# One loop for scan, z product and output product in the SSD layer of a two-layer transformer kernel

## The chip, the cores and the metric

The kernel runs on one core of one Trainium2 chip, for one sequence of 256 tokens with model width 2048, all data in 32 bit. The metric is the device time of one execution in microseconds (us), the median of several. The engines are TensorE (PE in the profile), VectorE (DVE), ScalarE (ACT), GpSimd (POOL), and the queue that starts the weight loads (SP).

## What is computed

Two layers follow each other: an attention layer with a Fourier part, then an SSD (state space) layer, a sparse attention layer on top of it and layer norms between. Only the SSD layer is touched. Its reference, cut:

```
def ssd_mixer(x, w_in, conv_w, conv_b, dt_bias, a_log, d_skip, norm_g, w_out):
    z, xbc, dt = jnp.split(x @ w_in, [4096, 4096 + 6144], -1)
    xs, bm, cm = split(silu(causal_depthwise_conv(xbc, conv_w, conv_b)))
    xs = xs.reshape(b, L, g, r, p)                 # 8 groups x 8 heads x 64
    dt = softplus(dt + dt_bias); a = -exp(a_log)
    y = ssd_chunked(xs, dt, a, bm, cm, chunk)      # one chunk of 256 tokens
    y = y + d_skip[..., None] * xs
    yg = (y * silu(z)).reshape(b, L, g, 512)
    yg = yg * rsqrt(mean(yg * yg, -1) + 1e-6)      # per group
    return (yg.reshape(b, L, 4096) * norm_g) @ w_out

def ssd_chunked(...):                              # with one chunk only y_diag is left
    cb = einsum('bclgn,bcsgn->bgcls', cc, bc)
    y_diag = einsum('bgcls,bgrcls,bcsgrp->bclgrp', cb, exp(segsum(dt * a)), xs * dt)
```

z (2048 to 4096 columns) needs only x; the scan of a group needs its x, B, C and dt columns; the output product of a group needs the scan and z of that group. So there are, for each of 8 groups, three pieces of work: one z block, one scan, one output block.

## The kernel before

Every weight matrix is streamed through SBUF once. A **tile** is 1 MB (512 rows by 512 columns) in one of four `raw` buffers, and has two **units** of 256 rows. Since TensorE multiplies in a shortened format, each unit is split into a high part `w_hi` (ScalarE, L402) and a low part `w_lo` (VectorE, L924), and TensorE does three products for each chunk: high by high, low by high, high by low (L1650 to L1652, 12 matmuls of 512 columns to a unit). Four units fit in `w_hi` and `w_lo`, so the split of unit u waits for `units_used` of u-4, and TensorE's unit u waits for `lo_done` of u. TensorE's order of work is written out by hand, and so are the orders of ScalarE and VectorE: between their own steps they are told to split so many units `ahead`, and each engine takes its instructions strictly in that order.

The stretch of interest has these stages:
- **dt product** (L1944) and, at its end, the z product: 8 blocks of 4 tiles (`z_block`, L1984), each 8 units, into PSUM banks 0 and 1 or 2 and 3 by turns. ScalarE reads each block with Silu (L718) into `gatedf`, where z of all 8 groups is kept.
- **scan loop** (`scan_turn`, L2013 on TensorE, L745 on ScalarE, L1303 on VectorE, `stage_scan`, L1609 on GpSimd), 8 turns. Turn g does the scan of group g and the output product of group g-1 (`out_tile`, four tiles of two units). On TensorE: the product C by B (`cb`, L2017, L2018), output tiles 0 and 1, the SSD product y (L2030 to L2032, 24 small matmuls, each done in two passes), output tiles 2 and 3, eight transposes of the normed y (L2042).
- after it four output tiles of group 7, and the layer norm.

Around y of group g stands a chain. ScalarE makes the decay factors in two halves, each 8 Relu instructions (L738) and one Exp of 1536 columns (L743); VectorE masks them (L1315) and weights x with dt (L1321) and with d_skip (L1333). When y is in PSUM, VectorE adds and gates it (L1342, L1345), ScalarE squares and sums (L757), VectorE forms the mean (L1348), ScalarE the root (L761), VectorE its inverse (L1350), ScalarE scales (L765), TensorE transposes, ScalarE and VectorE store the high and the low part (L771, L1356). VectorE also adds each output tile from PSUM to the residual x (`add_out`, L1301); out tile n may begin only after tile n-2 was added, for it has the same two banks. GpSimd brings the cumulated sums (`r`, a DMA of 1 MB broadcast, L1611) and stages the columns of B (L1618). ScalarE loads another function table when it goes from Silu or Sqrt to Exp and so on (ACT_TABLE_LOAD).

Of the kernel before, what the change touches and what calls it, by code (L numbers as in the profile page):

```python
# [83 lines left out]

def make_tables():
# [35 lines left out]
def tile_list():  # L121
# [16 lines left out]
    blocks("ssd_z", 8, 4)  # L138
    blocks("ssd_out", 32, 1)
# [12 lines left out]
def build(nc, a, out, acs_dram):  # L152
# [21 lines left out]
    for seg, _, _, _, _ in TILES:  # L174
        if seg not in ("head_q", "head_kv") and all(seg != s for s, _ in BLOCKS):
# [25 lines left out]
    with ExitStack() as ctx:  # L201
# [51 lines left out]
        def tile_source(seg, b, j):  # L253
# [88 lines left out]
        def _(sp):  # L342
# [50 lines left out]
        def _(e):  # L393
# [294 lines left out]
            def dt_splits(u0):  # L688
# [3 lines left out]
                e.activation(tx[0:64, 0:256], ps[0:64, 4, 0:256], ACT.Identity, bias=sm[0:64, 65:66]).then_inc(S["dt_act"], 1)  # L692
# [9 lines left out]
            def z_two(i):  # L702
                for k in range(2):
                    ahead = 2 * FIRST["ssd_z"] + 8 * k + 4
                    if k == 0 and isinstance(i, int):
                        dt_splits(ahead)
                    elif isinstance(i, int):

                        splits(ahead, 4)
                        e.activation(x[:, :, :], x[:, :, :], ACT.Copy, scale=ALPHA).then_inc(S["x_scaled"], 1)  # L710
                        splits(ahead + 4, 4)
                    else:
                        splits(ahead, 8, i, 16)
                    b = 2 * i + k
                    e.wait_ge(units_used, ready("ssd_z", b))
                    for n in range(2):
                        fixed()
                        e.activation(gatedf[:, ds(b * 1024 + LO + n * 512, 512)], ps[:, 2 * k + n, :],  # L718
                                     ACT.Silu).then_inc(act_freed if n == 1 else S["half_read"], 1)
            each(e, 4, z_two)  # L720


            ex = actf[:, 1024:4096]
            rb = actf[:, 5120:7168]
            U0 = 2 * FIRST["ssd_out"]
            e.wait_ge(units_used, ready("ssd_z", 7))
# [18 lines left out]
            def scan_turn(g):  # L745
                def ahead(m):
                    if not isinstance(g, int) or g > 0:
                        split(U0 - 8 + m, g, 8)

                decay(g, 1)  # L750
                for m in range(4, 8):
                    ahead(m)
# [22 lines left out]
                if not isinstance(g, int) or g < G - 1:  # L775
                    decay(g + 1, 0)
# [141 lines left out]
        def _(e):  # L918
# [384 lines left out]
            def scan_turn(g):  # L1303
                def ahead(m):
                    if not isinstance(g, int):
                        split(U0 - 8 + m, g, 8)

# [900 lines left out]
```

## Time and profile before

| | us |
|---|---|
| median of 3 runs | 2343.94 |
| lowest and highest | 2336.14 and 2345.91 |
| span of the profiled execution (first to last instruction) | 2338.8 |

The profile is that of one execution. For each engine it gives the busy time, the instructions in order of time with the wait before them and what ended it, and the clock that was granted to TensorE. "Idle" in brackets behind an instruction is the time its engine stood still before it, with the instruction that it waited for; "issue" is a wait for which the profile shows no releaser. The stretch from the first z unit to the last output unit goes from 1214.5 to 1671.4 us after the span's start, 456.9 us.

### The profile page before, as it was taken

The numbers are of one execution on the slowest core, as the hardware profiler recorded it, in microseconds if no ns is written. First come the engines' busy times: TensorE is split into PE (matmuls) and PEld (weight loads), VectorE is DVE, ScalarE is ACT, GpSimd is POOL, SyncE is SP. The second block draws the span as 40 slices with busy tenths as digits, with TensorE's granted clock in tenths as the row PEclk, the third lists the DMA queues.
The fourth block names the chain that finished last, engine by engine and source line by source line (L and its number), as shares of the span: only waits on it lengthen the run. The fifth ranks groups of instructions, "written<-read, shape, count | busy, mean of one in ns | idle before, by whom it ended". The sixth has DMA issues, their size and how long they took to land.

```text
span 2338.8 us, 33230 instructions
## 1 busy us (share of the span) xinstructions
PE 2144.7 (92%) x13270; PEld 1913.9 (82%) x13270; DVE 1359.4 (58%) x1772; ACT 1138.1 (49%) x1526; POOL 38.9 (2%) x60
## 2 busy tenths in 40 slices
PE   4989999999999998999999978999799998888996
PEld 3768898789999887999988867787698998776885
DVE  5864755444665555666664445777755544665454
ACT  5832445544553344444435446667454345564333
POOL 0000000000000000000000000010000000000000
PEclk8889999999999999999999998999899999999998
DMA  9933533335785554555545552445354554223652
GB/s 350 334 137 107 192 133 109 108 127 182 269 285 183 180 190 143 181 167 179 166 154 191 189 196 101 157 173 180 113 177 136 166 186 138 88 90 125 198 191 79
DMA packets 204233, 394.62 MB, mean 169 GB/s; under 512 B 6726, under 2 KB 25916, under 8 KB 201692
## 3 DMA queue, kind: packets, MB, share of 16 engines
q1 hardware_dynamic: 199584, 369.78, 47.4%
q0 software_dynamic: 2880, 17.40, 2.0%
q10 hardware_dynamic: 1660, 5.90, 0.6%
q8 instruction: 79, 1.29, 0.2%
q14 instruction: 30, 0.25, 0.0%
HBM read 390.89 MB, written 2.16 MB: 168 GB/s over the span
## 4 chain that ended last, share of the span: by engine, by line
PE 71%; ACT 10%; DVE 10%; issue 6%; DMA 1%; ACTq 1%; DVEq 0%; POOL 0%; POOLq 0%
PE ps L1662 11%; PE ps L1664 11%; PE ps L1663 11%; PE ps L1650 10%; PE ps L1651 10%; PE ps L1652 10%; ACT w_hi L402 4%; DVE w_lo L924 3%; ACT actf L738 2%; PE ps L1732 1%; PE ps L1733 1%; DMA tables<-in_tables 1%; ACT actf L859 1%; PE ps L1824 1%; DVE sm L1489 1%
## 5 line engine op out<-in xcount | busy, mean ns | idle before, releaser
L924 DVE TENSOR_TENSOR w_lo<-raw,w_hi 128x1024 fp32r<-128x1024 f32 (+1 forms) x708 | 850.3, 1220 | 765.5 <-ACT w_hi L402 764.9
L402 ACT ACTIVATE w_hi<-raw 128x1024 fp32r<-128x1024 f32 (+1 forms) x708 | 730.1, 1052 | 738.8 <-PE ps L1664 368.0
L1662 PE MATMUL ps<-act,w_hi 128*128 128x256 f32 x2048 | 587.3, 287 | 5.1 <-DVE w_lo L924 3.8
L1664 PE MATMUL ps<-act,w_lo 128*128 128x256 f32 x2048 | 580.8, 284 | 0.0
L1663 PE MATMUL ps<-act,w_hi 128*128 128x256 f32 x2048 | 580.7, 284 | 0.0
L1662 PEld LDWEIGHTS ps<-act,w_hi 128*128 128x128 f32 x2048 | 393.1, 192 | 9.6 <-DVE w_lo L924 4.6
L1663 PEld LDWEIGHTS ps<-act,w_hi 128*128 128x128 f32 x2048 | 393.0, 192 | 2.9 <-issue 2.2
L1664 PEld LDWEIGHTS ps<-act,w_lo 128*128 128x128 f32 x2048 | 392.9, 192 | 0.0
L1650 PE MATMUL ps<-w_hi,act 128*128 128x512 f32 (+1 forms) x896 | 354.1, 395 | 23.7 <-DVE act L1356 12.6
L1651 PE MATMUL ps<-w_lo,act 128*128 128x512 f32 (+1 forms) x896 | 349.3, 390 | 0.0
L1652 PE MATMUL ps<-w_hi,act 128*128 128x512 f32 (+1 forms) x896 | 349.2, 390 | 0.0
L1650 PEld LDWEIGHTS ps<-w_hi,act 128*128 128x128 f32 x896 | 170.2, 190 | 61.8 <-issue 25.7
L1651 PEld LDWEIGHTS ps<-w_lo,act 128*128 128x128 f32 x896 | 170.5, 190 | 34.4 <-issue 0.7
L1652 PEld LDWEIGHTS ps<-w_hi,act 128*128 128x128 f32 x896 | 170.1, 190 | 34.7
L1650 PE MATMUL ps<-w_hi,gated 128*128 128x512 f32 x320 | 126.7, 396 | 1.4 <-DVE gated L1520 1.4
L1651 PE MATMUL ps<-w_lo,gated 128*128 128x512 f32 x320 | 125.8, 393 | 0.0
L1652 PE MATMUL ps<-w_hi,gated 128*128 128x512 f32 x320 | 125.7, 393 | 0.0
L1732 PE MATMUL ps<-w_hi,gated 128*128 128x512 f32 x128 | 60.1, 469 | 21.9 <-DVE w_lo L924 21.8
L1662 PE MATMUL ps<-gated,w_hi 128*128 128x256 f32 x256 | 72.5, 283 | 3.7 <-DVE w_lo L924 3.7
L1650 PEld LDWEIGHTS ps<-w_hi,gated 128*128 128x128 f32 x320 | 61.0, 191 | 14.4 <-DVE gated L1520 1.6
L1663 PE MATMUL ps<-gated,w_hi 128*128 128x256 f32 x256 | 72.4, 283 | 0.0
L1664 PE MATMUL ps<-gated,w_lo 128*128 128x256 f32 x256 | 72.4, 283 | 0.0
(285 smaller groups left out, 2446.1 us busy)
## 6 DMA issues: line engine op xcount, KB each, us to landing
raw<-in_ssd_w_in SPq DMA_DIRECT2D x80, 1024.0 KB, 5.1
raw<-in_w_in SPq DMA_DIRECT2D x72, 1024.0 KB, 5.1
raw<-in_w_ada SPq DMA_DIRECT2D x48, 1024.0 KB, 5.8
raw<-in_dsa_w_in SPq DMA_DIRECT2D x36, 1024.0 KB, 5.0
raw<-in_ssd_w_out SPq DMA_DIRECT2D x32, 1024.0 KB, 5.0
raw<-in_dsa_w_out SPq DMA_DIRECT2D x32, 1024.0 KB, 5.1
raw<-in_w_out SPq DMA_DIRECT2D x16, 1024.0 KB, 5.1
raw<-in_w_proj_a SPq DMA_DIRECT2D x12, 1024.0 KB, 5.1
```

The lines of the kernel that those rows point to most:

```text
L402: e.activation(w_hi[:, u % SPLIT, :, :w], raw[:, t % RAW, 2 * h:2 * h + 2, :w], ACT.Copy).then_inc(hi_done, 1)
L738: ins = e.activation(ex[:, o:o + w], rb[:, h * 256 + tt * 128:h * 256 + 256], ACT.Relu, scale=-1.0, bias=sm[:, 76 + tt * 8 + h:77 + tt * 8 ...
L859: e.activation(v, v, ACT.Exp, bias=sm[:, c + 2 + tt:c + 3 + tt], scale=ATT_SCALE, accum_out=sm[:, c + 4 + tt:c + 5 + tt]).then_inc(S["hs_e ...
L924: e.tensor_tensor(w_lo[:, u % SPLIT, :, :w], raw[:, t % RAW, 2 * h:2 * h + 2, :w], w_hi[:, u % SPLIT, :, :w].bitcast(F32), ALU.subtract).t ...
L1489: e.tensor_reduce(sm[:, c + tt:c + 1 + tt], p[:, lo:hi], AX_X, ALU.max).then_inc(S["hs_step"], 1)
L1650: e.matmul(ps[:, bank, :w], hi, w_hi[:, slot, c, :w], start=first, stop=False)
L1651: e.matmul(ps[:, bank, :w], hi, w_lo[:, slot, c, :w], start=False, stop=False)
L1652: ins = e.matmul(ps[:, bank, :w], lo, w_hi[:, slot, c, :w], start=False, stop=last)
L1662: e.matmul(o, wh, hi, start=first and f % 2 == 0, stop=False, skip_group_check=True)
L1663: e.matmul(o, wh, lo, start=False, stop=False, skip_group_check=True)
L1664: ins = e.matmul(o, wl, hi, start=False, stop=last and f % 2 == 1, skip_group_check=True)
L1732: e.matmul(ps[:, bank + 2 * k, :], cols[:, kc, :], w_hi[:, slot, c, :], start=kc == 0, stop=False)
```

## The change

The 8 z blocks are no longer done ahead of the scan. Only z of groups 0 and 1 is (segment `ssd_z`, 2 blocks); then a loop of six turns (g = 1 to 6, two to a pass) does the scan of group g, the z block of group g+1 and the output product of group g-1, with one new run of weight tiles (`ssd_zo`: four z tiles, four output tiles); group 7's scan and the last two output products follow. z is kept for two groups only (`ZS`), and the room of the others takes the decay factors (`EX`), the broadcast sums (`RB`) and the low parts of y (`YL`). z is now always in banks 4 and 5, y in 6 and 7, `cb` in bank 0, which output tiles 0 and 2 have too. No arithmetic is added or left out. The same splits, products and DMAs are done; their order is another, and so is what each stands behind. New helper names are `z_silu`, `y_squares`, `y_root`, `y_scale`, `y_high` on ScalarE, `masked`, `weighted`, `y_gated`, `y_mean`, `y_rstd`, `y_low` on VectorE, and `group_products`, `y_product`, `y_turn` on TensorE: each holds the step of that name that the loop before had written out. `splits(u, n)` splits n units from u on.

The core of the diff:

```diff
+ZS = LO
+EX = LO + 2048
+RB = LO + 5120
+YL = 28
...
-    blocks("ssd_z", 8, 4)
-    blocks("ssd_out", 32, 1)
+    blocks("ssd_z", 2, 4)
+    blocks("ssd_zo", 6, 8)
+    blocks("ssd_out", 8, 1)
...
+            def scan_loads(i):
+                n0 = FIRST["ssd_zo"]
+                for j in range(4):
+                    load(n0 + j, i, i, 8)
                 for t in range(4):
-                    n = FIRST["ssd_out"] + t
-                    sp.wait_ge(lo_done, 2 * (n - RAW) + 2 + 8 * g)
-                    sp.dma_start(raw[:, n % RAW:n % RAW + 1, :, :],
-                                 w[:, ds(g, 1), :, t * CB:(t + 1) * CB]).then_inc(raw_landed[n % RAW], 16)
-            each(sp, G, out_group)
+                    out_tile(n0 + 4 + t, i, t, i, 8)
+            each(sp, 6, scan_loads)
+            for t in range(8):
+                out_tile(FIRST["ssd_out"] + t, 6 + t // 4, t % 4, 0, 0)
...
+            dt_splits(Z0 + 4)
+            z_silu(0, ready("ssd_z", 0))
+            splits(Z0 + 12, 4)
             decay(0, 0)
-            each(e, G - 1, scan_turn)
-            scan_turn(G - 1)
-            splits(U0 + 60, 8)
+            e.activation(x[:, :, :], x[:, :, :], ACT.Copy, scale=ALPHA).then_inc(S["x_scaled"], 1)
+            splits(Z0 + 16, 2)
+            decay(0, 1)
+            splits(Z0 + 18, 2)
+            z_silu(1, ready("ssd_z", 1))
+            y_squares(0)
+            y_root(0)
+            y_scale(0)
+            decay(1, 0)
+            decay(1, 1)
+            def scan_turn(g, k, i):
+                def ahead(m, n=1):
+                    splits(ZO + 16 * k + m, n, i, 32)
+                ahead(4, 4)
+                y_high(g - 1)
+                ahead(8, 4)
+                z_silu(k, ZO + 16 * k + 8 + 32 * i)
+                y_squares(g)
+                ahead(12)
+                y_root(g)
+                ahead(13)
+                y_scale(g)
+                ahead(14)
+                decay(g + 1, 0)
+                ahead(15)
+                ahead(16)
+                decay(g + 1, 1)
+                ahead(17, 3)
+            def scan_two(i):
+                scan_turn(2 * i + 1, 0, i)
+                scan_turn(2 * i + 2, 1, i)
+            each(e, 3, scan_two)
+            y_high(6)
+            splits(U0 + 4, 2)
+            y_squares(7)
+            y_root(7)
+            y_scale(7)
+            splits(U0 + 6, 4)
+            y_high(7, 4)
+            splits(U0 + 10, 10)
...
+            dt_splits(Z0 + 4)
+            splits(Z0 + 12, 8)
+            e.wait_ge(S["xt_copied"], 8)
+            e.wait_ge(S["acs_stored"], 16)
+            masked(0, 0)
+            masked(0, 1)
+            weighted(0)
+            y_gated(0, 0)
+            y_mean(0)
+            y_rstd(0)
+            e.wait_ge(S["x_scaled"], 1)
...
+            def scan_turn(g, k, i):
+                def ahead(m, n=1):
+                    splits(ZO + 16 * k + m, n, i, 32)
+                def add(t):
+                    e.wait_ge(units_used, ZO + 16 * k + 10 + 2 * t + 32 * i)
+                    e.wait_ge(dve_freed, out_freed(4 * g - 8 + t))
+                    v = x[:, :, t * 512:(t + 1) * 512]
+                    e.tensor_tensor(v, ps[:, 2 * (t % 2):2 * (t % 2) + 2, :], v, ALU.add).then_inc(dve_freed, 1)
+                masked(g, 0)
+                masked(g, 1)
+                ahead(4, 4)
+                weighted(g)
+                y_low(g - 1)
+                ahead(8, 4)
+                y_gated(g, (k + 1) % 2)
+                ahead(12)
+                y_mean(g)
+                ahead(13)
+                add(0)
+                y_rstd(g)
+                ahead(14, 2)
+                add(1)
+                ahead(16, 2)
+                add(2)
+                ahead(18, 2)
                 add(3)
...
+            masked(7, 0)
+            masked(7, 1)
+            weighted(7)
+            y_low(6)
+            splits(U0 + 4, 2)
+            y_gated(7, 1)
+            y_mean(7)
+            add_last(24)
+            y_rstd(7)
+            splits(U0 + 6, 2)
+            add_last(25)
+            splits(U0 + 8, 2)
+            add_last(26)
+            y_low(7, 4, 0)
+            splits(U0 + 10, 2)
+            add_last(27)
...
+            e.wait_ge(S["dt_ready"], 1)
+            e.wait_ge(S["xt_copied"], 8)
...
+            pair_free(BI["ssd_z"])
+            gemm(Z0, 8, act, 4, True)
+            turn_dt()
+            group_products(0)
+            e.wait_ge(act_freed, z_freed(0))
+            gemm(Z0 + 8, 8, act, 4, True)
+            y_product(0)
+            def scan_turn(g, k, i):
+                u0 = ZO + 16 * k
+                e.wait_ge(dve_freed, out_freed(4 * g - 6))
+                group_products(g)
+                e.wait_ge(act_freed, z_freed(g))
+                gemm(u0, 4, act, 4, True, i, 32, ends=False)
+                y_turn(g - 1)
+                gemm(u0 + 4, 4, act, 4, True, i, 32, kc0=8, starts=False)
+                y_product(g)
+                for t in range(4):
+                    out_tile(t, g - 1, u0 + 8, i, 32)
+            def scan_two(i):
+                scan_turn(2 * i + 1, 0, i)
+                scan_turn(2 * i + 2, 1, i)
+            each(e, 3, scan_two)
+            e.wait_ge(dve_freed, out_freed(22))
+            group_products(7)
+            y_turn(6)
+            y_product(7)
+            for t in range(3):
+                out_tile(t, 6, U0, 0, 0)
+            y_turn(7)
+            out_tile(3, 6, U0, 0, 0)
             for t in range(4):
-                out_tile(t, G)
+                out_tile(t, 7, U0 + 8, 0, 0, 4, 0)```

How it moves instructions, at three places.

On VectorE, the turn before from the gating of y to the third addition to x (L1345 gating, L924 `w_lo`, L1348 mean, L1350 inverse root, L1301 addition):

```order
L1345 TENSOR_TENSOR tables<-tables,gatedf 128x1024
L923 REGISTER_ALU
L924 TENSOR_TENSOR w_lo<-raw,w_hi 128x1024
L1347 ISA
L1348 TENSOR_SCALAR sm<-sm 128x2
L1349 REGISTER_ALU
L1350 RECIPROCAL sm<-sm 128x2
L923 REGISTER_ALU
L924 TENSOR_TENSOR w_lo<-raw,w_hi 128x1024
L1298 ISA
L1299 REGISTER_ALU
L1301 TENSOR_TENSOR x<-ps,x 128x2x512
```

and the turn now, from the gating (L1366) to the third addition (L1405 the addition, L980 `w_lo`, L1370 mean, L1374 inverse root):

```order
L1366 TENSOR_TENSOR tables<-tables,gatedf 128x1024
L980 TENSOR_TENSOR w_lo<-raw,w_hi 128x1024
L1370 TENSOR_SCALAR sm<-sm 128x2
L980 TENSOR_TENSOR w_lo<-raw,w_hi 128x1024
L1405 TENSOR_TENSOR x<-ps,x 128x2x512
L1374 RECIPROCAL sm<-sm 128x2
L980 TENSOR_TENSOR w_lo<-raw,w_hi 128x1024 x2
L1405 TENSOR_TENSOR x<-ps,x 128x2x512
L980 TENSOR_TENSOR w_lo<-raw,w_hi 128x1024 x2
L1405 TENSOR_TENSOR x<-ps,x 128x2x512
```

Before, two of the four additions stood ahead of the gating; now all four stand behind it, with six of the turn's `w_lo` among them.

On ScalarE, the turn before from behind the scaling of y to the next group's decay (L402 `w_hi`, L771 high part of y, L738 first Relu of the decay):

```order
L401 REGISTER_ALU
L402 ACTIVATE w_hi<-raw 128x1024
L767 REGISTER_ALU
L770 REGISTER_ALU
L771 ACTIVATE act<-ps,sm 128x256 x4
L401 REGISTER_ALU
L402 ACTIVATE w_hi<-raw 128x1024
L401 REGISTER_ALU
L402 ACTIVATE w_hi<-raw 128x1024
L731 ISA
L732 REGISTER_ALU
L738 ACTIVATE actf<-actf,sm 128x256
```

and now (L779 scaling, L433 `w_hi`, L756 Relu, L761 Exp):

```order
L779 ACTIVATE tables<-tables,sm 128x512 x2
L433 ACTIVATE w_hi<-raw 128x1024
L756 ACTIVATE gatedf<-gatedf,sm 128x256
...
L756 ACTIVATE gatedf<-gatedf,sm 128x128
L761 ACT_TABLE_LOAD
L761 ACTIVATE gatedf<-gatedf 128x1536
L433 ACTIVATE w_hi<-raw 128x1024 x2
L756 ACTIVATE gatedf<-gatedf,sm 128x256
```

The decay's first half came behind all of a turn's output units; now it stands between unit 14 and unit 15 of the turn's 16, and the second half between the first and the second unit of the next turn.

On TensorE, before, the end of the first z block (L1952 the transposes of dt, then z of the second):

```order
L1650 MATMUL ps<-w_hi,act 128x512
L1651 MATMUL ps<-w_lo,act 128x512
L1652 MATMUL ps<-w_hi,act 128x512
L1952 MATMUL ps<-tables 128x64 x4
L1650 MATMUL ps<-w_hi,act 128x512
```

and now (L2043 the transposes, L2085 and L2086 `cb` of group 0, L1741 z of group 1):

```order
L1743 MATMUL ps<-w_hi,act 128x512
L2043 MATMUL ps<-tables 128x64 x4
L2085 MATMUL ps<-side,tables 128x256
L2086 MATMUL ps<-side,tables 128x128
L1741 MATMUL ps<-w_hi,act 128x512
```

The product `cb` of group 0 came behind the eighth z block; now it comes ahead of the second one.

## Rows read from the trace of the kernel before

**Rows 1.** The page: busy time of the engines, and the chain that ended last.
```profile
PE 2144.7 (92%) x13270; PEld 1913.9 (82%) x13270; DVE 1359.4 (58%) x1772; ACT 1138.1 (49%) x1526; POOL 38.9 (2%) x60
...
PE 71%; ACT 10%; DVE 10%; issue 6%; DMA 1%; ACTq 1%; DVEq 0%; POOL 0%; POOLq 0%
```

**Rows 2.** Windows: length; busy PE, PEld, DVE, ACT, POOL; granted clock; DMA share, GB/s.
```profile
1214.50:1389.50 175.00, 174.99 (x773) 144.32 (x772) 82.25 (x74) 82.24 (x85) 0.56 (x1) 1.00 0.56 183
1389.50:1423.60 34.10, 15.15 (x64) 14.27 (x64) 11.41 (x13) 18.02 (x35) 4.36 (x7) 0.55 0.31 110
1423.60:1647.30 223.70, 208.57 (x1089) 177.12 (x1088) 164.31 (x170) 158.83 (x268) 16.71 (x27) 0.98 0.46 159
```

**Rows 3.** TensorE in order of time: start, length, instruction, idle before and its releaser.
```profile
1402.89 0.66 PE L2030 MATMUL ps<-actf 128*128 128x64 f32 x2 [7.95 <-DVE actf L1315]
...
1434.79 0.33 PE L2030 MATMUL ps<-actf 128*128 128x64 f32 x2
...
1440.06 0.48 PE L1650 MATMUL ps<-w_hi,act 128*128 128x512 f32 x1
...
1451.16 1.10 PE L2042 MATMUL ps<-tables 128*128 128x128 f32 x8
1452.09 0.60 PE L2017 MATMUL ps<-side,tables 128*128 x2
...
1455.37 0.49 PE L1650 MATMUL ps<-w_hi,act 128*128 128x512 f32 x1 [2.45 <-DVE act L1356]
...
1484.10 0.60 PE L2017 MATMUL ps<-side,tables 128*128 x2
```

**Rows 4.** ScalarE in order of time, from the squares of group 1.
```profile
1445.53 0.60 ACT L757 ACTIVATE ps<-tables 128x512 f32<-128x512 f32 x1 [8.52 <-DVE tables L1345]
...
1447.98 1.28 ACT L761 ACT_TABLE_LOAD   x1
...
1449.77 1.34 ACT L765 ACTIVATE tables<-tables,sm 128x512 f32<-128x512 f32 x2 [0.23 <-DVE sm L1350]
...
1455.28 2.88 ACT L738 ACTIVATE actf<-actf,sm 128x256 f32<-128x256 f32 x8
1458.17 1.28 ACT L743 ACT_TABLE_LOAD   x1
1459.47 1.49 ACT L743 ACTIVATE actf<-actf 128x1536 f32<-128x1536 f32 x1
1460.86 2.86 ACT L738 ACTIVATE actf<-actf,sm 128x256 f32<-128x256 f32 x8
...
1465.15 3.88 ACT L402 ACTIVATE w_hi<-raw 128x1024 fp32r<-128x1024 f32 x4
```

**Rows 5.** VectorE: the gating in order of time, then groups of 1452 to 1484.
```profile
1442.92 1.21 DVE L1342 TENSOR_TENSOR tables<-ps,tables 128x1024 f32<-128x1024 f32 x1
...
L924 DVE TENSOR_TENSOR w_lo<-raw,w_hi 128x1024 fp32r<-128x1024 f32 x8 | 9.5, 1216 | 4.8 <-ACT w_hi L402 4.8
L1301 DVE TENSOR_TENSOR x<-ps,x 128x1024 f32<-128x1024 f32 x4 | 4.9, 1214 | 0.0
L1315 DVE TENSOR_TENSOR actf<-actf,t 128x1536 f32<-128x1536 f32 x2 | 3.5, 1770 | 2.5 <-ACT actf L743 2.4
```

**Rows 6.** GpSimd in order of time: the first staging of B.
```profile
1390.06 0.59 POOL L1611 DMA_DIRECT2D actf<-acs_dram  x1 [159.80 <-PE ps L1652]
...
1391.84 1.39 POOL L1618 COPY tables<-side 128x256 f32<-128x256 f32 x1
```

**Rows 7.** VectorE's copy of dt, and ScalarE's scaling of x, in order of time.
```profile
1238.83 0.42 DVE L1273 COPY t<-ps 128x256 f32<-128x256 f32 x1
...
1249.06 3.61 ACT L710 ACTIVATE x<-x 128x4096 f32<-128x4096 f32 x1
```

**Rows 8.** Busy time and granted clock behind a wait of 2.46 us; columns as Rows 2.
```profile
1488.00:1490.00 2.00, 2.00 (x8) 1.60 (x7) 2.00 (x3) 2.00 (x7) 1.01 (x1) 0.70 0.95 371
1490.00:1492.00 2.00, 2.00 (x6) 1.52 (x6) 2.00 (x3) 1.97 (x3) 0.00 (x0) 0.50 0.27 30
```

More of the change, by code:

```diff
@@ L174, in build @@
     for seg, _, _, _, _ in TILES:
-        if seg not in ("head_q", "head_kv") and all(seg != s for s, _ in BLOCKS):
+        if seg == "ssd_zo" and all(seg != s for s, _ in BLOCKS):
+            for _ in range(6):
+                BLOCKS.append((seg, "act"))
+                BLOCKS.extend([(seg, "dve")] * 4)
+        elif seg not in ("head_q", "head_kv") and all(seg != s for s, _ in BLOCKS):
             nb = 1 + max(t[1] for t in TILES if t[0] == seg)
@@ L183, in build, with z_freed, out_freed @@
         BI.setdefault(seg, n)
+    Z_FREED = sum(1 for seg, who in BLOCKS[:BI["ssd_z"]] if who == "act")
+    OUT_FREED = sum(1 for seg, who in BLOCKS[:BI["ssd_z"]] if who == "dve")
+    def z_freed(b):
+        return Z_FREED + 1 + b
+    def out_freed(n):
+        return OUT_FREED + 1 + n
     def freed_count(engine, n):
@@ L282, in tile_source @@
                 return [(0, 4, rows(a["ssd_w_in_2"], k0, b * CB))]
+            if seg == "ssd_zo" and j < 4:
+                return [(0, 4, rows(a["ssd_w_in_2"], k0, b * CB + 2 * CB))]
             if seg == "lat_q":
@@ L700, in dt_splits, with z_silu @@
                 splits(u0 + 2, 6)
[L702 to L724, printed above, removed]
-            U0 = 2 * FIRST["ssd_out"]
-            e.wait_ge(units_used, ready("ssd_z", 7))
+            Z0 = 2 * FIRST["ssd_z"]
+            ZO = 2 * FIRST["ssd_zo"]
+            U0 = 2 * FIRST["ssd_out"]
+            ex = gatedf[:, EX:EX + 3072]
+            rb = gatedf[:, RB:RB + 2048]
+            def z_silu(k, used):
+                e.wait_ge(units_used, used)
+                for n in range(2):
+                    e.activation(gatedf[:, ZS + k * 1024 + n * 512:ZS + k * 1024 + (n + 1) * 512], ps[:, 4 + n, :],
+                                 ACT.Silu).then_inc(act_freed if n == 1 else S["half_read"], 1)
             def decay(g, n):
@@ L743, in decay, with y_squares @@
                 e.activation(part, part, ACT.Exp, scale=-1.0).then_inc(S["decay_ready"], 1)
[L745 to L752, printed above, removed]
+            def y_squares(g):
                 e.wait_ge(S["y_step"], 4 * g + 2)
@@ L1272, in dt_splits @@
                 e.wait_ge(S["dt_turned"], 1)
-                e.tensor_copy(t1[:, :], ps[:, 5, 0:256]).then_inc(S["dt_ready"], 1)
-            def z_two(i):
-                for k in range(2):
-                    ahead = 2 * FIRST["ssd_z"] + 8 * k + 4
-                    if k == 0 and isinstance(i, int):
-                        dt_splits(ahead)
-                    else:
-                        splits(ahead, 8, i, 16)
-            each(e, 4, z_two)
-            e.wait_ge(act_freed, freed("ssd_z", 7))
@@ L1303, in scan_turn @@
[L1303 to L1306, printed above, removed]
-                def add(t):
-                    if not isinstance(g, int):
-                        add_out(t, g)
-                def masked(n):
-                    e.wait_ge(S["decay_ready"], 2 * g + n + 1)
-                    v = ex[:, n * 1536:(n + 1) * 1536].rearrange("p (h l) -> p h l", h=4)
-                    e.tensor_tensor(v, v, cbm.unsqueeze(1).to_broadcast([P, 4, 384]), ALU.mult).then_inc(S["m_ready"], 1)
+                e.tensor_copy(t1[:, :], ps[:, 7, 0:256]).then_inc(S["dt_ready"], 1)
@@ L2013, in scan_turn, with group_products @@
[L2013 to L2014 removed]
+            Z0 = 2 * FIRST["ssd_z"]
+            ZO = 2 * FIRST["ssd_zo"]
+            U0 = 2 * FIRST["ssd_out"]
+            ex = gatedf[:, EX:EX + 3072]
+            bst = tx[:, 1024:1280]
+            def group_products(g):
                 e.wait_ge(S["b_staged"], g + 1)
                 e.wait_ge(S["cb_masked"], g)
[L2017 to L2018 removed]
+                e.matmul(ps[:, 0, 0:256], bst[:, 0:P], side[:, ds(256 * g + 2048, 256)], start=True, stop=True)
+                e.matmul(ps[:, 0, 256:384], bst[:, P:2 * P], side[:, ds(256 * g + 2048 + P, P)],
```

184 lines of the change are left out of this document (81 added, 103 removed).

## The prediction

> **What bounds the kernel now.** I read the page first, then busy time by windows, then the engines in order of time around the scan loop. On the page [rows 1] TensorE is busy for 92% of the span and is 71% of the chain that ended last: the reader is to see that only time in which TensorE waits, or runs at its lower clock, can be won or lost by a new order, since the change leaves all products as they are. The windows [rows 2] say where that time is. In the z blocks TensorE waits for nothing (174.99 of 175.00 us, clock 1.00): 8 blocks at 21.8 us, a unit (an eighth) 2.72 us. In the first scan turn (1389.5 to 1423.6) it works 15.2 of 34.1 us at a clock of 0.55; in the seven turns behind it 208.6 of 223.7 us. Output tiles are 12 matmuls to a unit like z, so 2.72 us too.
>
> A turn's own scan work on TensorE at full clock is y, 5.27 us (1434.79 to 1440.06), transposes 0.93 us (1451.16 to 1452.09), and `cb` about 0.87 us (from 1452.09 to the start of the 2.45 us of idleness ahead of 1455.37) [rows 3]: 7.07 us in all. From the first z unit to the last output unit there are 456.9 us; the work in it is 16 x 21.76 + 8 x 7.07 + 0.4 for dt = 405.1. **So 51.8 us are waits and half clock**: 34.1 - 7.1 = 27 in the first turn, 25 in the rest (a turn takes 32.0 us, 1452.09 to 1484.10 [rows 3], for 28.8 of work). The change can win at most these 51.8 us, and must not make others.
>
> **The chain of a turn now.** Let y of group g end at 0 on TensorE. I add what stands in ScalarE's and VectorE's queues, in the new order.
> - Gating, two VectorE instructions: from 1442.92 until ScalarE's squares at 1445.53 [rows 4, 5]: 2.6, so 2.7 with the hand-over.
> - Squares 1.4 (1445.53 to the split behind them): 4.2. `w_hi` 1.0: 5.2. Table load and root 1.6: 6.8. `w_hi` 1.0: 7.8.
> - Now VectorE: the new order has `w_lo` and addition 0 ahead of the inverse root, 1.14 each start to start (a row mean is 1.21 with its overlap [rows 5]), and 0.2: 10.3. Before, the inverse root followed at once (scaling began 1.79 after the load's start [rows 4]).
> - ScalarE: scaling 1.3, `w_hi` 1.0: 12.6. First half of the next decay 5.58 (1455.28 to 1460.86 [rows 4]): 18.2. `w_hi` of unit 15: 19.2. VectorE: `w_lo` of unit 15, then addition 1: **21.5**.
> - Output tile 3 has the banks of tile 1 and waits for addition 1. TensorE did tiles 0 to 2 in 6 x 2.72 = 16.3, so it **waits 5.2 us**. Tile 3 ends at 27.0.
> - ScalarE goes on: `w_hi` 20.2, second half of the decay 4.29 (1460.86 to 1465.15 [rows 4]) 24.5, `w_hi` 25.5; VectorE `w_lo`, addition 2: 27.8. The next `cb` uses bank 0 and waits for addition 2: **0.8 us** more.
> - Then TensorE has `cb` 0.87, a z block 21.76, transposes 0.93, y 5.27, with all units split in time (ScalarE needs 1.0 and VectorE 1.14 for one, TensorE 2.72): 28.8. The turn takes 27.8 + 28.8 = **56.6 us**.
>
> Before, the same two blocks and one scan took 32.0 + 21.8 = 53.8. TensorE's own work would be 50.6. So the z block does cover the transposes and the parts of y, but its cover lies on the wrong side: ScalarE is free during the z block and overbooked in the output tiles, where two decay halves and six splits queue behind the root. Six turns have 6 x 6.0 = 36.0 us of waits. Added up the same way, the old loop's turn comes to 32.2 us against 32.0 measured, so the sum is good to some tenths of a us in a turn.
>
> **Start.** z of group 0 ends at 1236.3 as before; dt's transposes are at 1236.7. `cb` of group 0 now stands ahead of z of group 1 and waits for the copy of dt (ends 1239.25 [rows 7]) and then GpSimd's first staging, 3.1 us (1390.06 to 1393.2 [rows 6]): until 1242.3, a wait of 5.5 us. Cover for it there is none. z of group 1 ends at 1264.9. VectorE must do 8 `w_lo` before it masks group 0, and the last of them wait for ScalarE, which from 1255.2 (split of unit 15) does decay 5.6, scaling of x 3.6 [rows 7], 2 splits, decay 4.3, 2 splits: 1272.6. Then `w_lo` 1.2, mask of `cb` 0.6, two masks at 1.7, two weightings at 1.14: 1280.2. y of group 0 **waits 15.4 us**. In turn 1 the units 4 to 7 of z come behind both decay halves of group 1 (ScalarE: root and scaling done 7.2 after y, decays 9.9, split 1.0, VectorE a mask 1.7 and `w_lo` 1.1: 20.9 from y to the unit), while TensorE has `cb`, four units and the transposes, 12.7, and some tenths of hand-over: **7.2 us**.
>
> **End.** `cb` 7 and the transposes of group 6 take 1.8 us, and no z block follows: VectorE still has two `w_lo`, addition 3, masks, weightings and low parts, so y of group 7 **waits 9.4 us** (from 1.8 to 11.2 behind `cb`: addition 2 at 0, 2 x 1.14, 1.14, 0.6, 3.4, 2.3, 1.6). Output tile 2 then waits 2.4 us for addition 24, which stands behind the gating, two splits and the mean.
>
> **Sum of waits at full clock:** 5.5 + 15.4 + 7.2 + 36.0 + 9.4 + 2.4 = 75.9 us.
>
> **Clock.** No row shows these waits, so I bound their clock from both sides. The nearest rows: behind 2.46 us of idleness the clock was 0.70 and then 0.50 in two windows of 2 us [rows 8], which costs 2 x (0.30 + 0.50) = 1.6 us, and 1.7 with the piece behind; behind 2.45 us at 1455.37 it stayed full [rows 2, 3]. And y of group 0, after 7.95 us of idleness, ran throughout at the half clock (its first step is 0.66 against 0.33), so 5.3 us more than 5.27. Least: the waits of 7 us and more alone fall to half, 2 x 5.3 for y of groups 0 and 7. Most: each wait costs 1.7 more. I take the upper end, since 5.2 us is twice the 2.46 that did cost it: start `cb` and z 2.5; y 0 with `cb` and z behind it 7.9; turn 1 1.7; in five more turns 1.7 less the 0.8 of slack that tile 3 has before addition 2, and a little for the second tile, 1.1 each, 5.5; y 7 and output 7.0. Sum **24.6** (least 10.6).
>
> A page of the Trainium skill, TensorE: Matmul & The Clock Gate, section "HAM oscillation — how this bites in real kernels", says that a loop with a wait in each iteration can find the clock fallen in each. By that rule all six turns would pay; by the rows about half did in the old loop.
>
> **Result.** Waits and half clock 75.9 + 24.6 = 100.5 against 51.8: **48.7 us slower**. The profiled execution's 2338.8 becomes 2387.5; the median shown is 5.1 above that span, so 2343.9 + 48.7 = **2392.6 us**. Silu's table load in each turn, the DMA (the same tiles in 56.6 us, each landing in about 5), and the copy of `r`, asked for some 19 us ahead, cost nothing: ScalarE is idle for 3.7 us before the squares, and the loads have two free buffers ahead.
>
> **Rivals.**
> 1. *The clock holds in the loop* (as at 1455.37): losses are 10.6 instead of 24.6: 2378.6, and 2368.0 with no loss at all. For it: half the old gaps lost nothing. Against it: these are twice as long. Chance 0.20, centred on 2379.
> 2. *The loop runs at TensorE's pace*, not slower than before: the place is addition 1 of VectorE; it decides by whether it is there 16.3 us after y, where I have 21.5. Then 36.0 and the 5.5 of clock in it are gone: 2392.6 - 41.5 = 2351.1, no change. For it: ScalarE and VectorE are busy some 34 of 50 us of a turn, so there is room on average. Against it: ScalarE's and VectorE's queues are in order, and each link of the 21.5 has its row. Chance 0.09.
> 3. *The same, and the clock holds too*: 75.9 - 36.0 = 39.9 against 51.8, 11.9 faster, 2332.0; and less if the start's 15.4 is shorter. Chance 0.08.
> 4. *Each table change costs more than its row.* On the chain there are two loads a turn (root, Exp). The row of a load is 1.28 and the next instruction starts 0.01 behind it (1458.17 to 1459.47 [rows 4]). If another 1.4 us, the length of the Exp's row, came with each of them, 16.8 in six turns would give 2409. The rows of both loads stand in the turn already, so 0.03.
>
> The Trainium skill's page ScalarE: Activation LUTs, section "What ACT_TABLE_LOAD costs", gives 1283 ns and a drain of some 1380 ns for each change of set; by it rival 4 would be the forecast. The trace agrees with the first figure and shows no second.
>
> **Chances.** The forecast has 0.60 (its own range 2383 to 2402), rivals 0.20, 0.09, 0.08, 0.03. Half a per cent, 11.7 us, is about what the measurement of this kernel tells from no change. Faster by more: rival 3, of which half lies at the limit and part of rival 2's spread, 0.08; within it: rival 2 and the rest, 0.10; slower 0.82. The range leaves out rival 3, part of rival 2 and what is above 2409: 2350 to 2409.
>
> **What would show it.** In the profile after: a turn of about 57 us from `cb` to `cb`; in each, TensorE idle by some 5 us before output tile 3, released by VectorE's addition to x, and again a little before `cb`; idle of 5.5 us behind z of group 0, of 15 us before y of group 0, of 9 before y of group 7; y of groups 0 and 7 at half clock. If tile 3 starts without a wait, the chain above is wrong and rival 2 or 3 holds. If the turn is 56 to 57 and the granted clock is 1.00 in the loop, rival 1. If ScalarE stands still behind a table load, rival 4.

## The result, and the profile after

The changed kernel takes 2395.1 us (median; 2393.75 to 2396.02), the kernel before, run beside it, 2344.9 us: a ratio of 1.0219, with a 95% interval of 1.0196 to 1.0241. It is slower by 50 us. The forecast was 2392.6 us.

Busy time of the engines on the page after, which answers to [rows 1]:

```profile
PE 2167.7 (91%) x13270; PEld 1932.6 (81%) x13270; DVE 1359.5 (57%) x1772; ACT 1148.6 (48%) x1533; POOL 36.2 (2%) x60
```

The same 13270 matmuls and 1772 VectorE instructions, and seven more on ScalarE (table loads). TensorE's 23.0 us more busy time at an equal count are matmuls at the lower clock. The rest of the loss is idleness, and the list of TensorE's waits from 1200 to 1760 us names it (engine, line, what it waited for: us in total, times, longest):

```profile
PE ps L1741 <- DVE x L1405: 29.6, 6, 5.0
PE ps L2100 <- DVE gatedf L1357: 15.2, 1, 15.2
...
PE ps L2100 <- DVE gated L1380: 10.0, 1, 10.0
PE ps L1741 <- DVE w_lo L980: 6.3, 1, 6.3
...
PE ps L2085 <- POOL tables L1709: 4.0, 1, 4.0
...
PE ps L1741 <- DVE x L1437: 2.2, 1, 2.2
```

L1741 is the first of a unit's products, L1405 and L1437 VectorE's additions to x, L2100 y, L2085 `cb`. From top to bottom these are: output tile 3 behind addition 1 in each of six turns; y of group 0 behind its weighting; y of group 7 behind the low parts of group 6; the fifth z unit of turn 1; `cb` of group 0 behind GpSimd's staging; output tile 2 of group 6.

Windows over the changed stretch, with the columns of [rows 2] (z of group 0; from there to y of group 0; y of group 0 and turn 1; turns 2 to 6, up to `cb` of group 7; the end):

```profile
1218.50:1241.00 22.50, 22.50 (x100) 18.05 (x98) 13.35 (x17) 11.38 (x14) 0.56 (x1) 1.00 0.38 121
1241.00:1286.00 45.00, 25.77 (x105) 20.83 (x106) 17.43 (x15) 27.11 (x35) 2.31 (x7) 0.80 0.51 175
1286.00:1363.90 77.90, 66.73 (x301) 57.03 (x302) 34.26 (x35) 46.71 (x76) 2.03 (x4) 0.83 0.29 96
1363.90:1653.20 289.30, 264.49 (x1262) 221.29 (x1261) 170.84 (x166) 170.92 (x250) 12.69 (x20) 0.94 0.49 165
1653.20:1725.00 71.80, 59.63 (x261) 50.27 (x259) 43.55 (x47) 24.04 (x32) 1.24 (x3) 0.83 0.44 149
```

Before, TensorE stood full and at a clock of 1.00 for 175 us of this stretch [rows 2]; after, only z of group 0 is so, and every other window has idleness and a clock below 1. From the first z unit to the last output unit there are now 506.1 us (1218.9 to 1725.0), against 456.9: **49.3 us more, where 48.7 was worked out**. The spans differ by 55.3; the other 6 us lie outside the changed stretch, 4.4 of them before it begins.

One turn, turn 2, in TensorE's order of time (`cb` of group 2, output tile 3, and `cb` of group 3):

```profile
1363.89 0.59 PE L2085 MATMUL ps<-side,tables 128*128 128x256 f32 x2
...
1414.01 0.80 PE L1741 MATMUL ps<-w_hi,gated 128*128 128x512 f32 x1 [4.84 <-DVE x L1405]
...
1421.46 0.59 PE L2085 MATMUL ps<-side,tables 128*128 x2
```

A turn is 57.6 us here, 57.8 to 58.0 in the four behind it. Tile 3 waited 4.84 us and took 7.45 us instead of 5.44, for it began at half clock (0.80 for its first product where 0.49 is usual). ScalarE in the same turn, from the squares:

```profile
1395.30 0.60 ACT L768 ACTIVATE ps<-tables 128x512 f32<-128x512 f32 x1 [4.37 <-DVE tables L1366]
...
1397.75 1.28 ACT L773 ACT_TABLE_LOAD   x1
...
1402.76 1.34 ACT L779 ACTIVATE tables<-tables,sm 128x512 f32<-128x512 f32 x2 [2.50 <-DVE sm L1374]
...
1404.95 2.87 ACT L756 ACTIVATE gatedf<-gatedf,sm 128x256 f32<-128x256 f32 x8
1407.84 1.28 ACT L761 ACT_TABLE_LOAD   x1
1409.13 1.48 ACT L761 ACTIVATE gatedf<-gatedf 128x1536 f32<-128x1536 f32 x1
1410.52 1.99 ACT L433 ACTIVATE w_hi<-raw 128x1024 fp32r<-128x1024 f32 x2
```

and VectorE behind it:

```profile
1411.59 1.23 DVE L980 TENSOR_TENSOR w_lo<-raw,w_hi 128x1024 fp32r<-128x1024 f32 x1 [5.29 <-ACT w_hi L433]
1412.74 1.22 DVE L1405 TENSOR_TENSOR x<-ps,x 128x1024 f32<-128x1024 f32 x1
```

Read from below: tile 3 starts at 1414.01, addition 1 ends at 1413.96, it stood behind the low split of unit 15, which stood behind the high split of unit 15, which stood behind the first half of the next group's decay, which stood behind the scaling, which waited 2.50 us for the inverse root, which stood behind a split and addition 0. No step of this is late because its work takes long; each is late for its place in a queue.

### The profile page after: what moved, and what is told of

It is laid out like the page before. It is cut to its first block, busy times and chain, and to the rows that moved or that the text cites. A ratio compares the mean times of both kernels' runs of the same rounds, so it can differ in the third digit from the quotient of the medians.

```text
span 2394.1 us, 32966 instructions
## 1 busy us (share of the span) xinstructions
PE 2167.7 (91%) x13270; PEld 1932.6 (81%) x13270; DVE 1359.5 (57%) x1772; ACT 1148.6 (48%) x1533; POOL 36.2 (2%) x60
## 3 DMA queue, kind: packets, MB, share of 16 engines
q8 instruction: 86, 1.41, 0.2%
## 4 chain that ended last, share of the span: by engine, by line
PE 72%; DVE 11%; ACT 10%; issue 5%; DMA 2%; ACTq 0%; DVEq 0%; POOL 0%; POOLq 0%; SPq 0%
PE ps L1753 11%; PE ps L1755 11%; PE ps L1754 11%; PE ps L1741 10%; PE ps L1742 10%; PE ps L1743 10%; ACT w_hi L433 4%; DVE w_lo L980 2%; ACT gatedf L756 1%; PE ps L1823 1%; DMA tables<-in_tables 1%; PE ps L1824 1%; ACT actf L915 1%; PE ps L1915 1%; PE ps L2100 1%
## 5 line engine op out<-in xcount | busy, mean ns | idle before, releaser
L980 DVE TENSOR_TENSOR w_lo<-raw,w_hi 128x1024 fp32r<-128x1024 f32 (+1 forms) x708 | 850.9, 1220 | 822.2 <-ACT w_hi L433 821.6
L433 ACT ACTIVATE w_hi<-raw 128x1024 fp32r<-128x1024 f32 (+1 forms) x708 | 731.4, 1051 | 797.1 <-PE ps L1743 403.2
L1741 PE MATMUL ps<-w_hi,act 128*128 128x512 f32 (+1 forms) x640 | 254.7, 398 | 13.7 <-issue 7.4
L1741 PE MATMUL ps<-w_hi,gated 128*128 128x512 f32 x576 | 234.7, 407 | 33.3 <-DVE x L1405 29.6
L1742 PE MATMUL ps<-w_lo,act 128*128 128x512 f32 (+1 forms) x640 | 250.8, 392 | 0.0
L1743 PE MATMUL ps<-w_hi,act 128*128 128x512 f32 (+1 forms) x640 | 250.5, 391 | 0.0
L1742 PE MATMUL ps<-w_lo,gated 128*128 128x512 f32 x576 | 231.0, 401 | 0.0
L1743 PE MATMUL ps<-w_hi,gated 128*128 128x512 f32 x576 | 230.3, 400 | 0.0
L1741 PEld LDWEIGHTS ps<-w_hi,gated 128*128 128x128 f32 x576 | 112.8, 196 | 59.9 <-issue 21.6
L1741 PEld LDWEIGHTS ps<-w_hi,act 128*128 128x128 f32 x640 | 123.0, 192 | 40.4 <-issue 10.0
L1743 PEld LDWEIGHTS ps<-w_hi,act 128*128 128x128 f32 x640 | 122.6, 192 | 25.1
L1742 PEld LDWEIGHTS ps<-w_lo,act 128*128 128x128 f32 x640 | 122.7, 192 | 24.7 <-issue 0.7
L1743 PEld LDWEIGHTS ps<-w_hi,gated 128*128 128x128 f32 x576 | 112.3, 195 | 24.6
L1742 PEld LDWEIGHTS ps<-w_lo,gated 128*128 128x128 f32 x576 | 112.9, 196 | 23.3
L1823 PE MATMUL ps<-w_hi,gated 128*128 128x512 f32 x128 | 59.9, 468 | 22.0 <-DVE w_lo L980 22.0
L1753 PE MATMUL ps<-gated,w_hi 128*128 128x256 f32 x256 | 73.3, 286 | 3.7 <-DVE w_lo L980 3.7
```

Source lines behind the costliest of these rows:

```text
L433: e.activation(w_hi[:, u % SPLIT, :, :w], raw[:, t % RAW, 2 * h:2 * h + 2, :w], ACT.Copy).then_inc(hi_done, 1)
L980: e.tensor_tensor(w_lo[:, u % SPLIT, :, :w], raw[:, t % RAW, 2 * h:2 * h + 2, :w], w_hi[:, u % SPLIT, :, :w].bitcast(F32), ALU.subtract).t ...
L1741: e.matmul(ps[:, bank, :w], hi, w_hi[:, slot, c, :w], start=first, stop=False)
L1742: e.matmul(ps[:, bank, :w], hi, w_lo[:, slot, c, :w], start=False, stop=False)
L1743: ins = e.matmul(ps[:, bank, :w], lo, w_hi[:, slot, c, :w], start=False, stop=last)
L1753: e.matmul(o, wh, hi, start=first and f % 2 == 0, stop=False, skip_group_check=True)
```

## The experiments

Each is the changed kernel with one thing moved (the last has all). "Stretch" is from the first z unit to the last output unit in the profile, 506.1 us in the changed kernel and 456.9 before; it leaves out what lies outside the change. The ratio is to the kernel before. Line numbers shift by some lines where a run's kernel is shorter or longer. Outside the stretch all ten kernels do the same work, and it took 1879.1 to 1888.0 us of the profiled spans, the most in the changed kernel; no run shows why. So the medians below fell by 2 to 7 us more than the stretches, and most of them lie under what was expected: the theories are read from the stretch and the turns.

**The decay last (e1).** ScalarE's loop:

```diff
-                ahead(14)
-                decay(g + 1, 0)
-                ahead(15)
-                ahead(16)
-                decay(g + 1, 1)
-                ahead(17, 3)
+                ahead(14, 6)
+                decay(g + 1, 0)
+                decay(g + 1, 1)
```

> Only ScalarE's order in the loop changes: both halves of the next group's decay come behind the turn's last split (unit 19) instead of between units 14, 15, 16 and 17. Theory (the turn is set by ScalarE's and VectorE's queues between y and the additions 1 and 2): addition 1 is there about 16 us after y, output tile 3 starts without a wait, the decays run while TensorE does the next z block, and only about 1.2 us of wait is left at the fifth z unit. A turn goes from 57.9 to about 51.8 us, the kernel to about 2362 us. Rival A (TensorE's two banks and the handing over of them cost the 5 us, whatever ScalarE does): the wait before tile 3 stays, about 2395. Rival B (the decays then come too late for y, and y waits for the masks): the turn stays at 57 to 58.

Measured: 2360.1 us, ratio 1.007 (1.0051 to 1.0088). Stretch 474.0, 32.1 less. A turn is 52.2 to 52.3 us. TensorE's waits:

```profile
PE ps L2097 <- DVE gated L1377: 15.3, 1, 15.3
PE ps L2097 <- DVE gatedf L1354: 15.2, 1, 15.2
PE ps L1738 <- DVE w_lo L977: 13.6, 6, 6.3
```

(L2097 is y here, L1738 the first of a unit's products.) The wait for the addition to x is gone from the list: the two banks alone cost nothing, so rival A falls. A smaller one, for the low split of the fifth z unit, stands in its place (13.6 us in six turns, 6.3 of them turn 1's as before), and y of group 7 waits 15.3 instead of 10.0, for its decay now comes later. Rival B falls as well.

**The inverse root first (e2).** VectorE's loop:

```diff
+                y_rstd(g)
                 ahead(13)
                 add(0)
-                y_rstd(g)
```

> Only VectorE's order in the loop changes: the inverse root stands right behind the mean, ahead of the low split of unit 13 and addition 0. ScalarE's scaling of y can start 2.3 to 2.5 us sooner. Theory (a chain on which every instruction counts): the turn goes from 57.9 to about 55.0 to 55.5 us, the kernel to about 2377 to 2380 us. Rival (only the decay's place counts, or there is slack in front of the scaling): a gain below 5 us.

Measured: 2369.9 us, ratio 1.011 (1.0092 to 1.0129). Stretch 486.5, 19.6 less; a turn 54.7 to 54.9. Moving one instruction of 0.15 us takes 3.1 us off a turn. What TensorE still waits for before tile 3:

```profile
PE ps L1741 <- DVE x L1405: 14.0, 6, 2.4
```

ScalarE's wait of 2.50 us for the inverse root is gone, and with it 2.5 us of the turn; the other 0.6 fit a shorter half clock. The clock still falls in each of the six turns, behind waits of 2.23 to 2.39 us, but tile 3 then works at half for 3.2 to 3.6 us and not for 4.1 to 4.6. The expectation was 2377 to 2380 us, 15 to 18 less; the stretch gives 19.6 and the median 25.2.

**Addition 1 between the splits (e3).**

```diff
-                ahead(14, 2)
+                ahead(14)
                 add(1)
+                ahead(15)
                 ahead(16, 2)
```

> Only VectorE's order changes: addition 1 stands between the low splits of units 14 and 15, so output tile 3 need not wait for the split of unit 15 to have its banks. Theory (two chains of equal length: behind addition 1 comes addition 2, which needs the second half of the decay and sets the next product of C and B): the wait before tile 3 falls below 1 us, and comes back in front of unit 15 and of the next turn's first product; turn 57.5 to 58, kernel 2394 to 2397 us. Rival (the wait for the banks is what costs): 5 us less a turn, kernel about 2365 us.

Measured: 2390.3 us, ratio 1.0203 (1.0183 to 1.0224). Stretch 506.5, the same within 0.4 us. Turns 2 to 6 take 59.2 us falling to 57.8, where 57.5 to 58 was expected, and turn 1 and the last group are shorter by as much. The waits have only changed places:

```profile
PE ps L2086 <- DVE x L1405: 27.1, 6, 4.7
PE ps L2101 <- DVE gatedf L1357: 15.2, 1, 15.2
PE ps L1742 <- DVE w_lo L980: 12.5, 7, 6.3
```

L2086 is `cb`: it now waits 27.1 us for addition 2, where tile 3 had waited 29.6 for addition 1; tile 3 waits 1.0 to 1.1 us, for the low split of unit 15. So there are two chains of nearly equal length, as the prediction had it, and releasing one gives nothing.

**Idle products in the wait (e4).**

```diff
-                for t in range(4):
+                for t in range(3):
                     out_tile(t, g - 1, u0 + 8, i, 32)
+                e.wait_ge(act_freed, z_freed(g + 1))
+                for n in range(16):
+                    e.matmul(ps[:, 4, :], act[:, 0, n, 0:P], act[:, 0, 0:2, :], start=True, stop=True)
+                out_tile(3, g - 1, u0 + 8, i, 32)
```

> TensorE gets 16 idle products (512 columns, their result is not used) ahead of output tile 3 in each of the six turns, 3.6 us in a wait of 5.0. Theory (the half clock in the loop costs about 1.2 us a turn beyond the 56.6 of the queues): the granted clock stays at 1.00 in the turns, a turn takes about 56.7 us, the kernel about 2388 us. Rival (the turn's 57.9 is the queues' own length and the clock is without effect, since tile 3 has slack): no change, 2395 us. If the idle products themselves delay tile 3: slower than 2395.

Measured: 2382.2 us, ratio 1.0162 (1.0143 to 1.0181): 12.9 us under the changed kernel's time, 8.7 in the stretch. A turn is 56.5 to 56.8 us. Windows around the wait, the changed kernel above and this one below (the third column from the right is the granted clock):

```profile
1409.00:1413.00 4.00, 0.17 (x1) 0.00 (x0) 1.41 (x2) 3.99 (x6) 0.00 (x0) 0.77 0.01 2
1413.00:1417.00 4.00, 3.00 (x7) 2.44 (x8) 2.08 (x2) 3.97 (x9) 0.00 (x0) 0.50 0.73 221
```
```profile
1406.00:1410.00 4.00, 4.00 (x19) 3.16 (x17) 0.99 (x1) 3.99 (x5) 0.00 (x0) 1.00 0.01 2
1410.00:1414.00 4.00, 2.78 (x12) 2.12 (x12) 2.50 (x3) 3.97 (x9) 0.00 (x0) 1.00 0.61 183
```

```profile
1468.30 0.49 PE L1741 MATMUL ps<-w_hi,gated 128*128 128x512 f32 x1 [1.38 <-DVE x L1405]
...
1474.70 0.69 PE L2085 MATMUL ps<-side,tables 128*128 x2 [0.66 <-DVE x L1405]
```

With work that nobody needs, the granted clock stays at 1.00 from turn 2 to turn 6, and TensorE shows what the queues alone make: behind the idle products a wait of 1.2 to 1.4 us is left before tile 3, and one of 0.4 to 0.7 before `cb`, which is the second chain's wait that the slow tile 3 had hidden. The half clock in the loop was worth 0.9 to 1.5 us a turn, 1.2 on average: 57.6 to 58.0 against 56.5 to 56.8. Of the 8.7 us of the stretch 5.9 are those five turns and 0.8 tile 3 of turn 1; the other 2.0 lie where nothing was changed, most of them at the fifth z unit of turn 1, which worked at half clock for 3.3 us instead of 6.3.

**The start's order (e5).** ScalarE and VectorE ahead of the loop:

```diff
-            splits(Z0 + 12, 4)
+            splits(Z0 + 12, 3)
             decay(0, 0)
-            e.activation(x[:, :, :], x[:, :, :], ACT.Copy, scale=ALPHA).then_inc(S["x_scaled"], 1)
-            splits(Z0 + 16, 2)
+            splits(Z0 + 15, 1)
             decay(0, 1)
+            splits(Z0 + 16, 2)
+            e.activation(x[:, :, :], x[:, :, :], ACT.Copy, scale=ALPHA).then_inc(S["x_scaled"], 1)
             splits(Z0 + 18, 2)
...
-            splits(Z0 + 12, 8)
+            splits(Z0 + 12, 3)
             e.wait_ge(S["xt_copied"], 8)
             e.wait_ge(S["acs_stored"], 16)
+            weighted(0)
+            splits(Z0 + 15, 1)
             masked(0, 0)
             masked(0, 1)
-            weighted(0)
+            splits(Z0 + 16, 4)
```

> Only the start changes, ahead of the loop. ScalarE does the two halves of group 0's decay behind the third and fourth split of the second z block, and the scaling of x behind them; VectorE weights group 0 and masks it before the low splits of units 16 to 19. Theory (y of group 0 waits 15.2 us for ScalarE's and VectorE's order, not for data): that wait nearly goes (below 3 us), and with it some of the half clock: about 18 us less, 2377 us. Rival (the wait is the arrival of the broadcast sums or of dt): the wait stays at 10 us or more.

Measured: 2375.4 us, ratio 1.0128 (1.0107 to 1.0149); stretch 489.4, 16.8 less. The wait of 15.2 us before y of group 0 has gone from the list of waits; one of 2.1 us for Silu's reading of banks 4 and 5 has come behind it, before z of group 2. The 15.2 us were order alone.

**`cb` of group 0 in the middle of the second z block (e6).**

```diff
-            group_products(0)
             e.wait_ge(act_freed, z_freed(0))
-            gemm(Z0 + 8, 8, act, 4, True)
+            gemm(Z0 + 8, 4, act, 4, True, ends=False)
+            group_products(0)
+            gemm(Z0 + 12, 4, act, 4, True, kc0=8, starts=False)
```

> Only TensorE's order at the start changes: the product of C and B of group 0 stands in the middle of the second z block instead of ahead of it. Theory: the 8 us between z of group 0 and this product go, but 3 us of them come back as the wait for Silu's reading of the same banks, and the next wait, before y of group 0, takes the rest except what it gained, so the end moves only by about 3 to 6 us: 2389 to 2392 us. Rival (waits add up, nothing gives back): 8 to 10 us less, 2386.

Measured: 2392.0 us, ratio 1.0211 (1.0194 to 1.0228); stretch 504.8, 1.3 less where 3 to 6 was expected; no difference from the changed kernel that the times can tell. From the first z unit to `cb` of group 1 it is 2.6 us shorter (74.6 for 77.2), and the rest is longer again by about half of that. The 4.0 us for GpSimd are gone, and the waits behind it are 3.2 us for Silu's reading of banks 4 and 5 and 14.5 instead of 15.2 before y. A wait that is followed by a longer one on another queue was worth almost nothing by itself here.

**The decay in its own turn's z block (e7).** ScalarE, and VectorE's masks likewise:

```diff
-                ahead(4, 4)
+                decay(g, 0)
+                ahead(4)
+                decay(g, 1)
+                ahead(5, 3)
                 y_high(g - 1)
...
-                ahead(14)
-                decay(g + 1, 0)
-                ahead(15)
-                ahead(16)
-                decay(g + 1, 1)
-                ahead(17, 3)
+                ahead(14, 6)
```

> The decay of group g moves from the output tiles of the turn before into its own turn's z block, its halves on both sides of the split of unit 4, and VectorE's masks likewise. Theory: TensorE waits for nothing in the loop, a turn takes its own work, 50.6 us; the first turn's 6 to 7 us wait goes too, the last group's y waits longer. Kernel about 2355 us, still slower than before (2345), since start and end keep theirs. Rival (masks come too late for y, or splits of z too late): turn 52 us or more.

Measured: 2345.3 us, ratio 1.001 (0.9999 to 1.0021); stretch 463.0, 43.2 less. Turns 2 to 6 are 50.6 us each, five times over, which is TensorE's own work to the tenth. ScalarE where the wait had been, waiting now for TensorE:

```profile
1489.61 1.99 ACT L433 ACTIVATE w_hi<-raw 128x1024 fp32r<-128x1024 f32 x2
1492.01 1.06 ACT L433 ACTIVATE w_hi<-raw 128x1024 fp32r<-128x1024 f32 x1 [0.41 <-PE ps L1742]
1494.73 1.06 ACT L433 ACTIVATE w_hi<-raw 128x1024 fp32r<-128x1024 f32 x1 [1.66 <-PE ps L1742]
```

This is 10 us under the 2355 of the expectation: turn 1 fell by 11.2 us (67.8 to 56.6, with waits of 2.6 for 6.3), and 6.6 us of the median lie outside the stretch. Even with turns 2 to 6 without a wait the joined form is only level with the kernel before. Beyond TensorE's own 405.1 us its stretch has 57.9 us, all of them ahead of turn 2 and behind turn 6; the old one has 51.8, of which 27 in its first turn.

**All together (e8).** e7, e2, e3 and e5; `cb` of group 0 in the middle of the second z block, which has banks 2 and 3 here; and at the end

```diff
             y_turn(6)
-            y_product(7)
-            for t in range(3):
+            e.wait_ge(S["cb_masked"], 8)
+            for t in range(2):
                 out_tile(t, 6, U0, 0, 0)
+            y_product(7)
+            out_tile(2, 6, U0, 0, 0)
```

with ScalarE's and VectorE's last turn in the order that fits.

> All together: decay in the z block, inverse root first, addition 1 between, the start's new order, the product of C and B in the middle of the second z block (which has banks 2 and 3, so that Silu's reading covers nothing), and at the end two output tiles of group 6 ahead of y of group 7, while its decay is made. Theory: waits left are 10 to 15 us (some in turn 1 and at the end) against the 51.8 of the kernel before: 2312 to 2320 us, faster than before by 1.0 to 1.4%. Rival (something not in the queues, as bandwidth or the clock, takes the gain back): 2335 us or more.

Measured: **2313.1 us, ratio 0.9871 (0.9854 to 0.9889)**, faster than both; stretch 428.8 against 405.1 of work. All that TensorE waits for in the stretch:

```profile
PE ps L1751 <- DVE gated L1384: 3.5, 1, 3.5
PE ps L1751 <- DVE x L1445: 3.4, 1, 3.4
PE ps L1751 <- DVE w_lo L980: 3.1, 2, 2.2
PE ps L2121 <- ACT tables L779: 1.6, 1, 1.6
PE ps L1751 <- ACT gatedf L743: 1.6, 1, 1.6
```

13.2 us, inside the 10 to 15 expected. The 51.8 of the kernel before, which the expectation sets against them, holds the half clock too: the figure like it is 23.7 (428.8 less 405.1), with the granted clock at half for about 20 us of this stretch. So the idea of the change was sound, z can cover the scan, and its order of instructions was what lost.

## Why the prediction was right, step by step

The sum came out at 48.7 us and the stretch at 49.3; the median at 2395.1 for 2392.6. By terms:

| step | worked out, us | profile after, us |
|---|---|---|
| `cb` of group 0 waits for GpSimd | 5.5 | 4.0, then at half clock |
| y of group 0 waits | 15.4 | 15.2 |
| fifth z unit of turn 1 waits | 7.2 | 6.3 |
| tile 3 waits, in each turn | 5.2 | 4.8 to 5.0 |
| `cb` waits for addition 2 | 0.8 | none; 0.4 to 0.7 with a full clock (e4) |
| a turn, with half clock | 57.7 | 57.6 to 58.0 |
| y of group 7 waits | 9.4 | 10.0 |
| output tile 2 of group 6 waits | 2.4 | 2.2 |
| y of groups 0 and 7 at half clock | yes | yes, 0.64 a step |

The chain behind y is shown, not only argued: taking one instruction out of it (e2), a block out of it (e1, e7) and freeing only one of its two ends (e3) moved the turns by 3.1, 5.6 and 7.3 us and, for e3, the stretch by nothing, where 2.4 to 2.9, 6.1, 7.3 and nothing were due.

Rival 1, that the clock holds, is answered by the rows and by e4: around tile 3 it was at half for 3.4 us in turn 1 and for 6.8 us in each of turns 2 to 6, and keeping it full there took 6.7 us off the stretch. The upper bound was the right one to take; the old loop's waits of 2.46 us lost the clock only in part of the turns, those of 4.8 in every one. The Trainium skill's page TensorE: Matmul & The Clock Gate, section "HAM oscillation — how this bites in real kernels", describes a clock that is found fallen in each iteration of a loop with a wait. This trace agrees, with six falls in six turns. Rivals 2 and 3 needed addition 1 within 16.3 us of y; it ended 21.3 us behind it (1392.7 to 1413.96). They describe e7, which is what that condition gives: turns of 50.6 us, and 2345.3 us where rival 2 had said 2351 with the waits of turn 1 left in. Rival 4, a dearer table change, falls: the Exp begins 0.01 us behind its load (1407.84 + 1.28 to 1409.13), the root 0.08 behind its own, and ahead of both loads ScalarE stands still for 0.02. The Trainium skill's page ScalarE: Activation LUTs, section "What ACT_TABLE_LOAD costs", adds a drain of some 1380 ns to each change of set; this trace shows none.

What was off, term by term, and what of the agreement is luck:

- *The first row.* `cb` began 1.75 us behind the copy of dt, which ended at 1243.64, and not 3.1. In the trace of [rows 6] GpSimd's two copies took 1.24 and 1.39 us, with VectorE at work beside them on a split and a weighting; here VectorE was idle:

```profile
1244.80 0.21 POOL L1705 COPY sm<-t 128x16 f32<-128x16 f32 x1
1244.93 0.41 POOL L1709 COPY tables<-side 128x256 f32<-128x256 f32 x1
```

  No run tests whether VectorE's work is the cause.
- *The third row.* Its own terms give 20.9 - 12.7 = 8.2 us, not 7.2; it measured 6.3, since TensorE, still at half clock behind y of group 0, needed 13.8 us for its part and the unit was split 20.2 us behind y. Turn 1 is 67.8 us, where the terms give 65.5, or 68.1 with the 2.6 us of half clock that the prediction puts down for `cb` and z behind y of group 0.
- *The fifth row* is a wait that could not show, since the slow tile 3 had used it up, as the sum allowed for in five turns (4.0 us of the 75.9 that its clock term takes off again).
- *Waits against clock.* The listed waits are 67.3 us where 71.9 were due (75.9 less those 4.0). All the rest beyond TensorE's own work, the half clock in the main, is 33.7 us (506.1 - 405.1 - 67.3) where 28.6 were due. The waits came out 4.6 us short and the rest 5.1 us long. That the two errors cancel to 0.6 us in the sum is luck; each of them alone would still have left the forecast within its range.
- *The medians.* Their agreement (2.5 us) is partly luck too, for TensorE reached the first z unit between 1214.3 and 1220.0 us in ten profiles of the same code ahead of it. Only the stretch itself can be compared to a microsecond.

## What to carry to other kernels

When work is moved under the cover of a busy engine, lay out for one turn which instructions each helper engine has during each part of the cover. An engine that is busy for 59% of a turn (ScalarE here, 34.2 of 57.9 us) can still be five microseconds late at one place, and an in-order queue hands that lateness to whatever stands behind it: here an addition that frees two banks. Work whose data were ready long before, like the decay here, belongs where its engine is idle and not behind the step that it follows in the formula; and of two waits in a row, or two chains of one length, removing one may show nothing (1.3 us in e6, none in e3).

## What the runs showed of the hardware

- The half clock lasted through a stretch in which TensorE was never idle. y of group 7 began after 9.96 us of idleness at 0.66 us for its first pair and still took 0.63 a pair in its last steps, 9 us later, with a granted clock of 0.50 from 1665 to 1675; the products of the output units behind it began at 1675.1 us with 0.77 and took their usual 0.40 from 1677.6.
- Products that nobody needs can pay: 16 of them in a wait of 5 us kept the granted clock at 1.00 and took 1.2 us off a turn on average, 6.7 us in six turns.
- Waits of one length can keep the clock or lose it: in the kernel before it held behind 2.45 us at 1455.37 and fell behind 2.46 [rows 8]; in e2 it fell behind six waits of 2.23 to 2.39 us.
- The same code ahead of the change differed by up to 5.7 us between ten profiles (1214.3 to 1220.0 us at the first z unit).
